# Expert weights in chunks of two neighbouring full-width rows for each partition, and the next expert's first weight between the second and the third

## What is computed

```python
aff = softmax(h @ w_router); gate, idx = top_k(aff per expert, cap)
xs = h[idx]                                     # 16 experts, 64 + 16 tokens each
hid = silu(xs @ w1) * (xs @ w3)                 # w1, w3: (1024, 1024) for each expert
ye = (hid @ w2) * gate                          # w2: (1024, 1024)
out[idx] += ye
```

## Time and profile before

| | |
|---|---|
| three runs | 3348.61, 3333.2, 3329.83 us, median 3333.2 us |
| the profiled execution's own time | 3351.13 us |
| its span, first to last instruction | 3349.3 us |
| mean granted TensorE clock | 0.936 |
| busy share: TensorE, VectorE, ScalarE, GpSimd | 89%, 58%, 44%, 12% |
| DMA | 595.34 MB in 373,481 packets |
| first layer's expert products | from 1084.65 to 1652.55 us |
| second layer's expert products | from 2746.79 to 3311.88 us |

### The profile page before, as it was taken

One profiled execution on the slowest core, in us unless ns is written; L12 is line 12 of the kernel. 1 busy time (PEld: TensorE's weight loads), 2 busy tenths in 40 slices (PEclk: granted clock), 3 DMA queues, 4 the chain that ended last, 5 costly groups with the idle time before them and its releaser, 6 DMA issues.

```text
span 3349.3 us, 40652 instructions
## 1 busy us (share of the span) xinstructions
PE 2983.2 (89%) x16648; PEld 2310.0 (69%) x16648; DVE 1942.1 (58%) x1787; ACT 1472.6 (44%) x1739; POOL 386.0 (12%) x237
## 2 busy tenths in 40 slices
PE   7988977899996999999788888879999959999996
PEld 6876765688884666666478767756888836666664
DVE  3277776311135888888543667763111368888884
ACT  4233333311124777777442333333111247777773
POOL 0421110000000111111122111100000000111110
PEclk9989988899998999999889889878999979999998
DMA  6221122112245999999812221121111259999995
GB/s 218 76 82 53 45 68 91 44 64 64 63 151 192 352 373 377 370 374 374 280 44 76 67 80 54 34 96 38 64 64 63 89 196 359 376 371 375 373 373 205
DMA packets 373481, 595.34 MB, mean 178 GB/s; under 512 B 12976, under 2 KB 164656, under 8 KB 373040
## 3 DMA queue, kind: packets, MB, share of 16 engines
q1 hardware_dynamic: 360208, 546.42, 46.3%
q0 software_dynamic: 13088, 46.28, 4.7%
HBM read 566.97 MB, written 25.69 MB: 177 GB/s over the span
## 4 chain that ended last, share of the span: by engine, by line
PE 65%; DVE 14%; DMA 12%; issue 4%; ACT 3%; POOL 2%; SPq 1%; DVEq 0%; POOLq 0%; ACTq 0%
PE ps L1146 15%; PE ps L1148 15%; PE ps L1147 15%; DMA m_raw<-in_w 10%; PE ps L1184 8%; PE ps L1308 2%; DVE m_lo L1083 2%; PE ps L1347 2%; POOL stats L437 2%; DVE stats L944 2%; DVE zc L912 2%; PE ps L1338 1%; PE ps L1393 1%; PE ps L1221 1%; DVE qk_b L931 1%
## 5 line engine op out<-in xcount | busy, mean ns | idle before, releaser
L755 ACT CAST m_hi<-m_raw 128x2048 fp32r<-128x2048 f32 x384 | 732.9, 1911 | 319.8 <-DMA m_raw<-in_w 270.2
L1083 DVE TENSOR_TENSOR m_lo<-m_raw,m_hi 128x2048 fp32r<-128x2048 f32 x384 | 861.8, 2284 | 18.5 <-PE ps L1148 12.9
L1146 PE MATMUL ps<-h_hi,w_hi 128*128 128x320 f32 x1408 | 448.5, 319 | 43.6 <-DVE h_lo L872 19.0
L1147 PE MATMUL ps<-h_lo,w_hi 128*128 128x320 f32 x1408 | 441.3, 313 | 0.0
L1148 PE MATMUL ps<-h_hi,w_lo 128*128 128x320 f32 x1408 | 441.1, 313 | 0.0
L1146 PE MATMUL ps<-m_hi,xs_hi 128*80 128x512 f32 x1024 | 406.6, 397 | 8.8 <-DVE xs_lo L1100 8.8
L1147 PE MATMUL ps<-m_lo,xs_hi 128*80 128x512 f32 x1024 | 404.3, 395 | 0.0
L1148 PE MATMUL ps<-m_hi,xs_lo 128*80 128x512 f32 x1024 | 403.5, 394 | 0.0
L827 DVE TENSOR_TENSOR w_lo<-raw,w_hi 128x2048 fp32r<-128x2048 f32 x68 | 157.9, 2323 | 368.7 <-ACT w_hi L536 344.8
L536 ACT CAST w_hi<-raw 128x2048 fp32r<-128x2048 f32 x48 | 91.2, 1903 | 528.4 <-DMA raw<-in_w_gate 333.8
L1146 PEld LDWEIGHTS ps<-h_hi,w_hi 128*128 128x128 f32 x1408 | 269.9, 192 | 51.4 <-issue 49.8
(11 more groups left out here) (239 smaller groups left out, 4533.0 us busy)
## 6 DMA issues: line engine op xcount, KB each, us to landing
m_raw<-in_w SPq DMA_DIRECT2D x384, 1024.0 KB, 10.3
raw<-in_w_in SPq DMA_DIRECT2D x72, 512.0 KB, 5.0
raw<-in_w_ada SPq DMA_DIRECT2D x64, 512.0 KB, 4.7
raw<-in_w_gate SPq DMA_DIRECT2D x48, 512.0 KB, 5.5
ada_in_a<-in_w_ada SPq DMA_DIRECT2D x10, 1024.0 KB, 12.5
raw<-in_w_proj_a SPq DMA_DIRECT2D x16, 512.0 KB, 4.4
raw<-in_w_out SPq DMA_DIRECT2D x16, 512.0 KB, 5.0
moe_rows<-zeros POOLq DMA_DIRECT2D x10, 512.0 KB, 6.8
```

Source lines behind the costliest of these rows:

```text
L755: nc.scalar.copy(m_hi[:, g % HIS], m_raw[:, g % RAWS]).then_inc(s["m_high"], 1)
L1083: nc.vector.tensor_tensor(m_lo[:, g % LOS], m_raw[:, g % RAWS], m_hi[:, g % HIS].bitcast(F32), ALU.subtract).then_inc(s["msplit"], 1)
L1146: pe.matmul(out, wh, xh, start=first, stop=False, skip_group_check=True)
L1147: pe.matmul(out, wh, xl, start=False, stop=False, skip_group_check=True)
```

## The change

A chunk is now two neighbouring rows of full width for each partition: the row index is split as `(p k)`, partition p holds rows 8p to 8p+7, and chunk k of a weight has rows 8p+2k and 8p+2k+1, which are 8 KB of neighbouring memory. The number of chunks, their bytes and the slots stay. To fit the new order of rows, the transposes of the tokens and of `hid` take every eighth column: column 8p+k of a row goes to partition p, tile k.

Each product runs over two row tiles and both column halves, so the matmuls change the PSUM bank after every three. A weight's two halves are complete together, so silu, `gate_up`, the turn of `hid` and its split happen once for each expert, on 1024 columns.

The order is w1(0), w3(0), then for each expert: w1 of the next expert, w2 of this one, w3 of the next. `hid` of expert e is turned after the second chunk of w1(e+1) (for the last expert right after its w3); the rows of expert e+2 are turned after the first chunk of w2(e), those of expert 1 after the very first chunk. `xs_hi` and `xs_lo` are double, and all transposes write PSUM banks 6 and 7. TensorE waits for silu of the expert before ahead of a new w1. ScalarE's silu and `expert_out` now stand behind the `high` of five chunks on.

```diff
-CHUNKS = [(0, 0, 0, 0), (0, 4, 0, 0), (1, 0, 0, 1), (1, 4, 0, 1), (0, 0, 1, 2), (0, 4, 1, 2), (1, 0, 1, 3), (1, 4, 1, 3),
-          (2, 0, 0, 4), (2, 0, 1, 5), (2, 4, 0, 4), (2, 4, 1, 5)]
-NCH = len(CHUNKS)
-CHUNKS_ALL = EXPERTS * NCH
+SPAN = 2
+CHUNKS = [(0, 0, k) for k in range(4)]
+for _e in range(EXPERTS):
+    CHUNKS += [(_e, 1, k) for k in range(4)]
+    CHUNKS += [(_e + 1, 0, k) for k in range(4) if _e < EXPERTS - 1]
+    CHUNKS += [(_e, 2, k) for k in range(4)]
+CHUNKS_ALL = len(CHUNKS)
+AFTER = {key: n + 1 for n, key in enumerate(CHUNKS)}
+TURN_HID = {AFTER[(e + 1, 0, 1) if e < EXPERTS - 1 else (e, 1, 3)]: e for e in range(EXPERTS)}
+TURN_ROWS = {AFTER[(e, 2, 0)]: e + 2 for e in range(EXPERTS - 2)}
...
-            ex_v = [w.rearrange("l e (k p) n -> l e p k n", p=P) for w in (w1, w3, w2)]
+            ex_v = [w.rearrange("l e (p k) n -> l e p k n", p=P) for w in (w1, w3, w2)]
...
-                for g in range(CHUNKS_ALL):
-                    e, n = divmod(g, NCH)
-                    w, k, c, _ = CHUNKS[n]
+                for g, (e, w, k) in enumerate(CHUNKS):
                     if g >= RAWS:
                         sp.wait_ge(s["msplit"], seen("msplit", 0) + g - RAWS + 1)
                         seen.settle()
-                    sp.dma_start(m_raw[:, g % RAWS], ex_v[w][l, e][:, k:k + EK, c * EW:(c + 1) * EW]).then_inc(s[f"mfull{g % RAWS}"], 16)
+                    sp.dma_start(m_raw[:, g % RAWS], ex_v[w][l, e][:, SPAN * k:SPAN * (k + 1), :]).then_inc(s[f"mfull{g % RAWS}"], 16)
...
                 gather(0)
+                pool.wait_ge(s["xs_ps"], seen("xs_ps"))
+                gather(1)
                 for e in range(EXPERTS):
-                    pool.wait_ge(s["xs_ps"], seen("xs_ps"))
                     if e < EXPERTS - 1:
-                        gather(e + 1)
+                        pool.wait_ge(s["xs_ps"], seen("xs_ps"))
+                    if e < EXPERTS - 2:
+                        gather(e + 2)
                     pool.wait_ge(s["ye_r"], seen("ye_r"))
...
+                    act.wait_ge(s["mdone"], seen("mdone", 0) + AFTER[e, 0, 3])
+                    nc.scalar.activation(hid[:], flat[0:SLOTS, 0:FF], ACT.Silu).then_inc(s["silu"], 1)
...
+                    nc.scalar.copy(ht_hi[:], ps[:, 6:8, :].rearrange("p b (k n) -> p (b k) n", k=4)[:, :, 0:SLOTS]).then_inc(s["ht_high"], 1)
...
+                    nc.scalar.copy(xs_hi[e % 2][:], ps[:, 6:8, :].rearrange("p b (k n) -> p (b k) n", k=4)[:, :, 0:SLOTS]).then_inc(s["xs_high"], 1)
...
-                    act.wait_ge(s["mdone"], seen("mdone", 0) + (e + 1) * NCH)
+                    act.wait_ge(s["mdone"], seen("mdone", 0) + AFTER[e, 2, 3])
...
-                rows_high()
-                for e in range(EXPERTS):
-                    for n in range(NCH):
-                        g = e * NCH + n + AHEAD_HI
-                        if g < CHUNKS_ALL:
-                            high(g)
-                        if n == 1:
-                            silu(e, 0)
-                        if n == 5:
-                            turned_high(0)
-                            silu(e, 1)
-                        if n == 8:
-                            turned_high(1)
-                        if n == 9 and e < EXPERTS - 1:
-                            rows_high()
-                    expert_out(e)
+                rows_high(0)
+                for n in range(CHUNKS_ALL + 1):
+                    if n in TURN_HID:
+                        turned_high()
+                    if n + AHEAD_HI < CHUNKS_ALL:
+                        high(n + AHEAD_HI)
+                    if n == 2:
+                        rows_high(1)
+                    if n in TURN_ROWS:
+                        rows_high(TURN_ROWS[n])
+                    if n and CHUNKS[n - 1][1:] == (0, 3):
+                        silu(CHUNKS[n - 1][0])
+                    if n and CHUNKS[n - 1][1:] == (2, 3):
+                        expert_out(CHUNKS[n - 1][0])
...
+                    dve.wait_ge(s["mdone"], seen("mdone", 0) + AFTER[e, 1, 3])
+                    nc.vector.tensor_tensor(hid[:], hid[:], flat[0:SLOTS, 2 * 512:4 * 512], ALU.mult).then_inc(s["hidd"], 1)
...
-                rows_low()
-                for e in range(EXPERTS):
-                    for n in range(NCH):
-                        g = e * NCH + n + AHEAD_LO
-                        if n == 6:
-                            turned_low(0)
-                        if n == 9:
-                            turned_low(1)
-                        if n == 10 and e < EXPERTS - 1:
-                            rows_low()
-                        if g < CHUNKS_ALL:
-                            low(g)
-                        if n == 3:
-                            gate_up(e, 0)
-                        if n == 7:
-                            gate_up(e, 1)
+                rows_low(0)
+                for n in range(CHUNKS_ALL):
+                    if n and CHUNKS[n - 1][1:] == (1, 3):
+                        gate_up(CHUNKS[n - 1][0])
+                    if n in TURN_HID:
+                        turned_low()
+                    if n + AHEAD_LO < CHUNKS_ALL:
+                        low(n + AHEAD_LO)
+                    if n == 2:
+                        rows_low(1)
+                    if n in TURN_ROWS:
+                        rows_low(TURN_ROWS[n])
...
-                        ins = pe.transpose(flat[:, 2 * 512 + k * P:2 * 512 + k * P + SLOTS], xg[:, k * P:(k + 1) * P], ident[0:SLOTS, 0:SLOTS])
+                        ins = pe.transpose(flat[:, 6 * 512 + k * P:6 * 512 + k * P + SLOTS], xg[:].rearrange("s (p k) -> s k p", k=KT)[:, k], ident[0:SLOTS, 0:SLOTS])
...
                 def product(n):
 
-                    w, k0, c, bank = CHUNKS[n % NCH]
-                    hi, lo = (xs_hi, xs_lo) if w < 2 else (ht_hi, ht_lo)
+                    e, w, kp = CHUNKS[n]
+                    hi, lo = (xs_hi[e % 2], xs_lo[e % 2]) if w < 2 else (ht_hi, ht_lo)
                     pe.wait_ge(s["msplit"], seen("msplit"))
-                    for k in range(EK):
-                        ins = three(ps[0:SLOTS, bank, :], hi[:, k0 + k, :], lo[:, k0 + k, :], m_hi[:, n % HIS, k, :], m_lo[:, n % LOS, k, :],
-                                    k0 + k == 0, k0 + k == KT - 1)
+                    for j in range(SPAN):
+                        k = SPAN * kp + j
+                        for c in range(2):
+                            ins = three(ps[0:SLOTS, 2 * w + c, :], hi[:, k, :], lo[:, k, :], m_hi[:, n % HIS, j, c * 512:(c + 1) * 512],
+                                        m_lo[:, n % LOS, j, c * 512:(c + 1) * 512], k == 0, k == KT - 1)
                     ins.then_inc(s["mdone"], 1)
...
+                    for k in range(KT):
+                        ins = pe.transpose(flat[:, 6 * 512 + k * P:6 * 512 + k * P + SLOTS], hid[:].rearrange("s (p k) -> s k p", k=KT)[:, k], ident[0:SLOTS, 0:SLOTS])
...
-                for e in range(EXPERTS):
-                    pe.wait_ge(s["xs_out"], seen("xs_out"))
-                    for n in range(NCH):
-                        if n == 8:
-                            pe.wait_ge(s["ht_out"], seen("ht_out"))
-                            if e:
-                                pe.wait_ge(s["ye_r"], seen("ye_r"))
-                        if n == 10:
-                            pe.wait_ge(s["ht_out"], seen("ht_out"))
-                        product(e * NCH + n)
-                        if n == 5:
-                            turn_hid(0)
-                        if n == 8:
-                            turn_hid(1)
-                        if n == 9 and e < EXPERTS - 1:
-                            turn_rows()
+                for n, (e, w, k) in enumerate(CHUNKS):
+                    if (w, k) == (0, 0):
+                        pe.wait_ge(s["xs_out"], seen("xs_out"))
+                        if e:
+                            pe.wait_ge(s["silu"], seen("silu"))
+                    if (w, k) == (2, 0):
+                        pe.wait_ge(s["ht_out"], seen("ht_out"))
+                        if e:
+                            pe.wait_ge(s["ye_r"], seen("ye_r"))
+                    product(n)
+                    if n == 0 or n + 1 in TURN_ROWS:
+                        turn_rows()
+                    if n + 1 in TURN_HID:
+                        turn_hid()
```

More of the change, by code:

```diff
@@ L43 @@
 Q0, K0, V0, POOL0, CONVA0, CONVB0 = 0, 1024, 2048, 3072, 3584, 4096
-EW = 512
-EK = 4
 RAWS, HIS, LOS = 6, 6, 4
 AHEAD_HI, AHEAD_LO = 5, 3
-CHUNKS = [(0, 0, 0, 0), (0, 4, 0, 0), (1, 0, 0, 1), (1, 4, 0, 1), (0, 0, 1, 2), (0, 4, 1, 2), (1, 0, 1, 3), (1, 4, 1, 3),
-          (2, 0, 0, 4), (2, 0, 1, 5), (2, 4, 0, 4), (2, 4, 1, 5)]
-NCH = len(CHUNKS)
-CHUNKS_ALL = EXPERTS * NCH
+SPAN = 2
[8 more added lines that the diff above has]
+TURN_ROWS = {AFTER[(e, 2, 0)]: e + 2 for e in range(EXPERTS - 2)}
 MERGE = [(q, b) for q in range(2) for b in (1, 0, 2)]
@@ L174, in build @@
         xg = sb("xg", [SLOTS, D], r_m)
```

(46 more changed lines are left out.)

## The result

The kernel after took 3350.28 us (median of 20 runs, 3336.08 to 3362.01) against 3333.51 for the one before on the same chips (20 runs): ratio 1.0038, 95% interval 1.0024 to 1.0052. By the interval it is 0.24% to 0.52% slower, some 13 us, on the edge of what I had called no change. I had forecast 1.4 us less. The time lies within my range, but its sign was wrong.

A forecast was written before the change was run, and what follows sets the result against it. TensorE and the DMA engines were both taken as full, TensorE paying through small steps behind landings. Excess -33.8, end +8.4 and strided loads +24 gave -1.4 us: 3333.2 to 3332 us, range 3302 to 3376.

The forecast's parts named there:

- The DMA wait: Expert-stage chunk loads: 8 KB pieces reach an estimated 396 GB/s against 374, so the pipe no longer sets the pace.
- rival B: Expert-stage loads: the pipe stays the bound at 374 GB/s, experts stay at 35.3 us; 3342 us, chance 0.10.
- the new place of `hid`: `hid` turned two products after w3 and needed two later: TensorE's waits for `hid_t_lo` and `hid` both go.
- Queues passed: ScalarE's silu and `expert_out` behind one more `high`, then scatter and gather: cost 0, with 3.5 us of slack.
- rival D: Gather of token rows is late behind 8 KB pieces, using up the 3.5 us of slack: 3353 us, chance 0.06.
- The floor of 34.20 us: TensorE's need for one expert, 144 matmuls and 16 transposes, read from the second expert of each layer.
- A change of bank costs nothing: Expert products changing PSUM bank after every three matmuls: 0, as the projection chunks showed.
- The strided transposes: Transposes reading columns 32 bytes apart load at half pace: 0.37 us for each of 64 groups, +24 us.
- Rival A: Transposes: the strided loads cost nothing; 3308 us, chance 0.31.
- rival C: Transposes: strided loads run at a quarter of the pace, 1.1 us a group, 71 in all; 3379 us, chance 0.11.
- The open end: Last expert of each layer, no next w1 to hide behind: 3.2 us waiting plus 1.0 half clock, +8.4 in all.
- -33.8: Expert stage: the whole excess of 15 experts a layer over 34.20 us each, 18.4 + 15.4, booked as won.

The follow-up runs named there:

- e4: Kernel after with 4 KB pieces, transposes from neighbouring addresses, and rows turned later (edits of e2 and e3 together): 3316.71 us, ratio 0.9939 to before.
- e1: Kernel after with the old 2 KB chunks, old split of rows and contiguous transposes, keeping new order and merged small steps: 3340.69 us, ratio 1.0020 to before.
- e5: e3 with rows 8p+k and 8p+k+4 in one chunk, so 4 KB pieces with the stride kept: 3334.1 us, ratio 1.0004 to before.
- e3: Kernel after with rows turned four products later, those of expert 1 three products later: 3335.79 us, ratio 1.0001 to before.
- e2: Kernel after with full-width chunks of two row tiles, 4 KB pieces, and transposes from neighbouring addresses: 3321.28 us, ratio 0.9955 to before.
- e6: e4 with its two inner loops exchanged, six matmuls to a PSUM bank in place of three: one run, 3320.9 us.
- e7: e4 with the last expert's w3 ahead of the w2 of the one before it, filling the open end: 3307.66 us, ratio 0.9916 to before.

## Why the prediction was wrong

**The DMA wait: right.** The whole run's ScalarE wait for landings fell from 270.2 us to 39.7, TensorE's waits for `hid_t_lo` and `hid` are gone but for the last expert's, and rival B (the pipe stays the bound) is refuted: TensorE is full at 377 GB/s, and at 385 in e4. How much more the pipe could carry, 396 or not, no run shows. What I had credited with the end of those two waits, the new place of `hid`, doesn't do it by itself: e1 has that place, and TensorE waits for `hid_t_lo` as often as before. And the change's own size, 8 KB, was not needed; 4 KB did it.

**The step that failed: "Queues passed ... Cost 0, with 3.5 us of slack".** I priced the scatter and the gather behind it by rows of before and said of rival D that "a less crowded pipe should land it earlier than 9.0". The opposite came. The chain of the kernel after (start us, us, what) has the gather for expert 1, then an ordinary scatter with the gather behind it:

```profile
1075.85 10.38 DMA xg<-h_rows,token_of_slot
...
1274.01 10.71 DMA moe_rows<-ye,token_of_slot
...
1284.98 3.35 POOL xg L486
```

From a scatter's issue to the next gather's I had 9.64 us from the earlier trace rows; here it is 1284.98 - 1274.01 = 10.97. The landing takes 10.7 in place of 9.0, at most 12.7. Together 3.0 us of the 3.5 are used at the median, and the longer ones come late. The other links held, by the medians of the trace: from the end of w2 to the scatter's issue 3.45 us where I had 3.3, and from the end of w2 to the turn of the rows 25.85 where I had 25.5. For expert 1 I had set "3.8 for a quiet gather"; it lands after 10.38 in a pipe that isn't quiet. In one order of work, both steps grow with the piece of the load, as the first three lines of the table show (the third has strided loads besides). e5 and e3, both with strided loads and the rows turned late, differ in the piece and not in the stride, and show the same:

| pieces | GpSimd's wait for a scatter, mean of 26, us | gather's landing, median, us |
|---|---|---|
| 2 KB (e1) | 6.5 | 8.8 |
| 4 KB (e2) | 7.2 | 10.4 |
| 8 KB (after) | 7.9 | 10.7 |
| 4 KB (e5) | 7.0 | 11.3 |
| 8 KB (e3) | 7.7 | 12.2 |

The stride is not the cause: e4, contiguous with 4 KB, has 6.8 and 11.6, close to e5. Why longer pieces hold the small transfers up, no run shows. The price is the 10.8 us that e3 wins back in the first and middle groups. That is rival D, to which I gave 0.06: its mechanism was the right one, and at e3's ratio the forecast of no change would have held.

**The floor of 34.20 us: too low.** I took two undisturbed experts of the old order as what TensorE needs. With full-width chunks and a bank change after every three matmuls, contiguous groups never go below 34.39 (e4), because the products stand 231.0 ns apart against 229.7 in the early expert of the earlier trace rows. Over 30 groups that is 6 us. The new order alone is not all of it: e1, with the old chunks and a bank change after twelve, has groups 2 to 5 of the first layer at 34.25 to 34.38 us, their products 230.0 to 230.6 ns apart. "A change of bank costs nothing" was part of it: in e6 six matmuls to a bank win 0.4 of the 1.4 ns, some 2 us, by the bank or by the order of operands. The projection chunks of the earlier trace rows differed by 0.01 us over 42 matmuls, 0.2 ns each, which I had rounded to nothing. What makes up the rest stays open; before, too, had 229.9 to 231.7 in its later experts.

**The strided transposes: mechanism right, term too large.** I had 0.37 us for a group of 8 and 24 us in all; it is 0.30 a group (0.61 / 2), 64 x 0.30 = 19.5. A load lasts 206 ns in place of 140, and transposes start 111 ns apart in place of 69: 42 ns more, where I had 53. I had said that TensorE "has no cycle to spare"; but 69 ns are 166 cycles at 2.4 GHz for 128 columns. Rival A (no cost) and rival C (a quarter of the pace, 1.1 us a group) are both refuted. The Trainium skill, Advanced Engine Details and Errata, section Memory Cachelines, which gives a penalty for another 16-byte line at each access, has the trace on its side here: 42 ns for 128 columns at 32 bytes.

**The open end: right, a little larger.** Forecast 4.2 us a layer; filling it in e7 won 77.5 - 67.6 = 9.9 in both, 5.0 each. The waiting was sized well, 1.38 + 1.64 = 3.0 us against 3.2, but the half clock was not: the 11 matmuls from 1636.81 to 1641.59 take 4.78 us where 11 x 0.231 = 2.54, so 2.2 and not 1.0.

The sum with measured terms: -33.8 + 6 (floor) + 19.5 (stride) + 9.9 (end) + 10.8 (gathers) = +12.4 us. The profiled stages differ by 10.6 and the ratio gives 13: it closes within some 2 us. Against my own sum the floor is 6 worse, the stride 4.5 better and the end 1.5 worse; that these three leave only 3 us together is luck. The late gathers, which I had called nothing, are the rest, and they turned no change into a loss.

## What to carry to other kernels

When a transfer is made faster, look at every small transfer that shares the DMA engines: its landing here grew with the neighbours' pieces, and slack that is counted by old landings is not slack. Take the layout that is contiguous for the consumer as well (4 KB rows gave all the bandwidth that TensorE could use and none of the strided loads), and test the size in the middle before the largest. An order that overlaps experts has an end with nothing to overlap; filling it was worth 9.9 us here, as much as 0.3 us in each of the 32 experts.

## What the runs showed that I had not expected

- Small indirect transfers get slower while the DMA engines get less busy: at a DMA share of 1.05 with 2 KB pieces (e1) a gather lands in 8.8 us, at 1.01 with 8 KB (after) in 10.7.
- An idle time of 1.34 us before the rows of expert 1 was followed by eight transposes and three matmuls at a granted clock of 1.00 and then by 3.7 us at 0.54; in the first layer, after 1.04 us, the clock stayed at 1.00 (1086.30 to 1110).
- Weight loads of 128 columns 32 bytes apart cost neither twice nor four times the contiguous load, but 1.5 times (206 against 140 ns).
